# A two-block fp32 transformer kernel on one core: the start reordered, with the stream loaded ahead of the modulation weights and lambda computed first

## The reference, cut to what matters

```python
c_act = jax.nn.silu(c)
mod = c_act @ mod_w[i] + mod_b[i]                     # 1024 -> 6144
sh_m, sc_m, gt_m, sh_f, sc_f, gt_f = jnp.split(mod, 6)
h = rmsnorm(x, norm_pre_mix[i]) * (1.0 + sc_m) + sh_m
y = conformer_conv_module(h, a_pw1_w, ...)            # h @ w1 first: 1024 -> 2048
...
hdn = jnp.sin(freq * (z @ fw1 + fb1))                 # z: 1024 x 33, fw1: 33 x 64
hdn = jnp.sin(freq * (hdn @ fw2 + fb2))               # fw2: 64 x 64
...
lam = exp(sum(lambda_q1 * lambda_k1)) - exp(sum(lambda_q2 * lambda_k2)) + lam_init
a = p[:, :, 0] - lam * p[:, :, 1]                     # in the attention
```

## Time and profile before

| | |
|---|---|
| median of 3 runs | 3311.95 us |
| lowest and highest | 3311.55 and 3317.38 us |
| the profiled execution | 3311.95 us |
| its span | 3310.2 us |
| mean granted TensorE clock | 0.963 of full |
| PE busy | 3096.4 us |
| DVE, ACT, POOL busy | 1656.5, 1011.4, 433.0 us |
| span start to the first pw1 matmul | 61.1 us |

### The profile page before, as it was taken

The page is one execution under the profiler, slowest core; times in us unless marked ns, Lnnn a source line. Parts: engine busy times, 40 slices in busy tenths (PEclk is TensorE's granted clock), DMA queues, the critical chain, the costliest instruction groups (busy, mean ns, idle before and its releaser), DMA issues. The chain is left out here.

```text
span 3310.2 us, 33559 instructions
## 1 busy us (share of the span) xinstructions
PE 3096.4 (94%) x13822; PEld 2500.5 (76%) x13822; DVE 1656.5 (50%) x1752; ACT 1011.4 (31%) x1203; POOL 433.0 (13%) x177
## 2 busy tenths in 40 slices
PE   7897878899999999989999999889999999999996
PEld 3683457778888888768888877678777788888885
DVE  5596765665556564574521066577465413222225
ACT  3444434232222121233221133467232311111111
POOL 0587750000000000000200034000020000000000
PEclk9998888899999999999999999999998999999998
DMA  6113432132323322221332244442332212111112
GB/s 206 51 39 121 159 121 102 64 103 76 91 63 127 102 92 81 102 77 64 124 123 94 99 153 143 118 91 54 105 113 73 75 32 64 45 42 61 39 45 108
DMA packets 96192, 301.24 MB, mean 91 GB/s; under 512 B 11205, under 2 KB 15045, under 8 KB 95847
## 3 DMA queue, kind: packets, MB, share of 16 engines
q1 hardware_dynamic: 96040, 299.09, 27.6%
HBM read 251.34 MB, written 47.71 MB: 90 GB/s over the span
## 5 line engine op out<-in xcount | busy, mean ns | idle before, releaser
L704 PE MATMUL ps<-mainr,wh 128*128 128x512 f32 (+1 forms) x6592 | 1778.5, 390 | 28.8 <-POOL wl L2445 9.7
L704 PEld LDWEIGHTS ps<-mainr,wh 128*128 128x128 f32 x6592 | 1236.5, 189 | 284.4 <-issue 28.0
L704 PE MATMUL ps<-mainr,wl 128*128 128x512 f32 (+1 forms) x3296 | 1029.0, 389 | 0.0
L704 PEld LDWEIGHTS ps<-mainr,wl 128*128 128x128 f32 x3296 | 622.4, 189 | 128.0
L1238 ACT CAST wh<-raw 128x1024 fp32r<-128x1024 f32 (+2 forms) x320 | 281.9, 885 | 749.7 <-PE ps L704 539.0
L1714 DVE TENSOR_TENSOR wl<-raw,wh 128x1024 fp32r<-128x1024 f32 (+2 forms) x256 | 265.4, 1038 | 462.8 <-ACT wh L1238 462.6
L2445 POOL TENSOR_TENSOR wl<-raw,wh 128x1024 fp32r<-128x1024 f32 x64 | 154.2, 2415 | 426.1 <-ACT wh L1238 425.9
L1973 DVE TENSOR_TENSOR mainf<-mainf,ps 128x1024 f32<-128x1024 f32 x80 | 97.6, 1220 | 214.5 <-PE ps L704 214.5
L750 PE MATMUL ps<-mainr,wh 128*128 128x512 f32 x576 | 163.0, 406 | 36.8 <-issue 22.2
L2016 DVE SCALAR_TENSOR_TENSOR ps<-mainf,vec,ps 128x1024 f32<-128x1024 f32 (+1 forms) x174 | 180.9, 1102 | 2.5 <-ACT ps L1426 2.3
L2483 POOL TENSOR_TENSOR tmp<-tmp,mainf 128x1024 f32<-128x1024 f32 x8 | 27.5, 3442 | 1177.0 <-DMA mainf<-in_rope 1114.9
(11 more groups left out here) (232 smaller groups left out, 2872.3 us busy)
## 6 DMA issues: line engine op xcount, KB each, us to landing
raw<-in_mod_w SPq DMA_DIRECT2D x48, 512.0 KB, 4.3
raw<-in_ada_w SPq DMA_DIRECT2D x48, 512.0 KB, 3.6
raw<-in_f_up SPq DMA_DIRECT2D x44, 512.0 KB, 4.3
raw<-in_g_up SPq DMA_DIRECT2D x44, 512.0 KB, 3.5
raw<-in_w_in SPq DMA_DIRECT2D x40, 512.0 KB, 4.1
raw<-in_pw SPq DMA_DIRECT2D x24, 512.0 KB, 3.9
sc_x<-mainf SPq DMA_DIRECT2D x24, 512.0 KB, 2.6
mainf<-sc_x SPq DMA_DIRECT2D x24, 512.0 KB, 6.2
```

The costliest lines, as they stand in the source:

```text
L704: ins = e.matmul(out, wt[:, a:b], xs[n], start=kk == 0 and t == 0, stop=kk == kt - 1 and t == 2)
```

## The change

The orders of all engines but POOL are changed.

- SP: x is issued right after vec and ident, then dbias and lamv; the raw tiles 0 to 3 come behind them. zT, fw1, fw2 and fsmall come after raw tile 11, whose issue waits for raw tile 7 to be consumed.
- PE: blocks 0 and 1, hidden layer 0, block 2, the sums of squares, turns 0 to 2, block 3, turn 3, hidden layer 1, the spread.
- ACT: the two exponentials of lambda come ahead of the squares of x, rows 0 to 2 after them, then the root, row 3, the first sine, the first three weights of pw1.
- DVE: all of lambda comes ahead of the additions of squares; sums 0 to 2 stand together, sum 3 after xxcopy and ahead of the reciprocal; hidden_argument(1) after the reciprocal.
- Planner: the first hidden layer and the column sums are taken ahead of block 3.

The number of instructions of each kind stays as it is, apart from waits and table loads.

```diff
--- before.py
+++ after.py
@@ -540,10 +540,11 @@
         d, acc, tmp = self.d, self.acc, self.tmp
         for i in range(1, ND):
             tmp.take(("x1sq", i), ("x1add", i))
-        for jb in range(4):
+        for jb in range(3):
             self.mod_paired("m", jb)
         self.aux_take(("hid", 0), [("hts", 0)], [("hts", 0)])
         self.aux[0].take(("cols", "x1"), ("sqrt", "n1"), ("xxcopy",))
+        self.mod_paired("m", 3)
         self.aux_take(("hid", 1), [("hts", 1)], [("hts", 1)])
         self.norm_plan("n1")
         acc.only(0, 1, 2)
@@ -942,19 +943,18 @@
 
 
     modulation("m", 0)
+    modulation("m", 1)
     hidden_layer(0)
-    modulation("m", 1)
-    modulation_turn("m", 0)
+    modulation("m", 2)
     w.wait_ge(*k.at("ones", 0))
     w.wait_ge(*k.at("x1add", ND - 1))
     columns(k.S(0), True, True, "x1", 0)
-    modulation("m", 2)
-    modulation_turn("m", 1)
+    for jb in range(3):
+        modulation_turn("m", jb)
+    modulation("m", 3)
+    modulation_turn("m", 3)
     hidden_layer(1)
-    modulation("m", 3)
-    modulation_turn("m", 2)
     norm_spread("n1")
-    modulation_turn("m", 3)
 
 
     x, ready = normed("n1", 8, 16)
@@ -1396,19 +1396,20 @@
     w.wait_ge(*k.at("vec", 0))
     e.activation(k.COL("cact", 0, 8), k.V("c1", 0, 8), ACT.Silu).then_inc(*k.to("cact", 0))
     e.activation(k.COL("cact2", 0, 16), k.V("c2", 0, 16), ACT.Silu).then_inc(*k.to("cact", 1))
+    for n in range(2):
+        w.wait_ge(*k.at("lamsum", n))
+        e.activation(k.COL("lam", n), k.COL("lam", n), ACT.Exp).then_inc(*k.to("lamexp", n))
     for i in range(ND):
         w.wait_ge(*k.at(f"x{i}", "x"))
         if i:
             hold_tmp("x1sq", i)
         e.activation(k.TMP("x1sq", i) if i else k.S(0), k.F(i), ACT.Square).then_inc(*k.to("x1sq", i))
-        if i == 3:
-            modulation_row("m", 0)
-    modulation_row("m", 1)
+    for jb in range(3):
+        modulation_row("m", jb)
     root(("n1",), RMS_EPS, ("cols", "x1", 0))
+    modulation_row("m", 3)
     hidden_sine(0)
-    modulation_row("m", 2)
     split_to(k.W["pw1", 0] + 3)
-    modulation_row("m", 3)
     norm_upper("n1", lambda i: k.R(8 + i), lambda i: k.COL("mod", i))
 
 
@@ -1449,9 +1450,6 @@
             split_to(k.W["pw1", 2 * i + 1] + 3)
         if i == 0:
             hidden_sine(1)
-            for n in range(2):
-                w.wait_ge(*k.at("lamsum", n))
-                e.activation(k.COL("lam", n), k.COL("lam", n), ACT.Exp).then_inc(*k.to("lamexp", n))
         products(POOL_TAPS[i] // 2)
         for t in FIRST_TAPS[i]:
             first_tap(t)
@@ -2085,6 +2083,16 @@
     e.memset(k.COL("sq", 0, 16), 1.0 / 1024).then_inc(*k.to("sq1"))
     for n, v in enumerate(m.eps):
         e.memset(m.eps[v], v).then_inc(*k.to("eps", n))
+    w.wait_ge(*k.at("lam", 0))
+    for n in range(2):
+        pr = m.lamv[:, 128 * n:128 * n + 64]
+        e.tensor_tensor(pr, pr, m.lamv[:, 128 * n + 64:128 * n + 128], ALU.mult).then_inc(*k.to("lammul", n))
+        w.wait_ge(*k.at("lammul", n))
+        e.tensor_reduce(k.COL("lam", n), pr, AX.X, ALU.add).then_inc(*k.to("lamsum", n))
+    w.wait_ge(*k.at("lamexp", 1))
+    e.tensor_tensor(k.COL("nlam"), k.COL("lam", 1), k.COL("lam", 0), ALU.subtract).then_inc(*k.to("nlam", 0))
+    w.wait_ge(*k.at("nlam", 0))
+    e.tensor_scalar(k.COL("nlam"), k.COL("nlam"), -LAM_INIT, None, ALU.add).then_inc(*k.to("nlam", 1))
     for i in range(1, ND):
         w.wait_ge(*k.at("x1sq", i))
         if i > 1:
@@ -2094,16 +2102,16 @@
     hidden_argument(0)
     hidden_reduce(0)
     w.wait_ge(*k.at("vec", 0))
-    modulation_add("m", 0)
+    for jb in range(3):
+        modulation_add("m", jb)
     w.wait_ge(*k.at("cols", "x1", 0))
     w.wait_ge(*k.at("sqrt", "n1"))
     e.tensor_copy(k.COL("xx", 0, 8), m.ps[:, 3072:3080]).then_inc(*k.to("xxcopy"))
+    modulation_add("m", 3)
+    w.wait_ge(*k.at("ident", 0))
     scale(("n1",))
-    modulation_add("m", 1)
+    split_to(k.W["pw1", 0] + 3)
     hidden_argument(1)
-    modulation_add("m", 2)
-    split_to(k.W["pw1", 0] + 3)
-    modulation_add("m", 3)
     hold_mod("m", 3)
     gain(k.COL("gm", 0, 8), k.COL("mod", 8, 8), k.V("npm", 0, 8), "n1")
     norm("n1", lambda i: k.F(i), lambda i: [(f"x{i}", "x")], lambda i: k.COL("mod", i), 8, 16)
@@ -2111,12 +2119,6 @@
 
     turns = vector_turns()
     hidden_reduce(1)
-    w.wait_ge(*k.at("lam", 0))
-    for n in range(2):
-        pr = m.lamv[:, 128 * n:128 * n + 64]
-        e.tensor_tensor(pr, pr, m.lamv[:, 128 * n + 64:128 * n + 128], ALU.mult).then_inc(*k.to("lammul", n))
-        w.wait_ge(*k.at("lammul", n))
-        e.tensor_reduce(k.COL("lam", n), pr, AX.X, ALU.add).then_inc(*k.to("lamsum", n))
     abreast_weights(("pw1", 0))
     for i in range(ND):
         for n in range(2):
@@ -2353,10 +2355,6 @@
         e.scalar_tensor_tensor(out=e1, in0=e1, scalar=k.STAT(n, 5), in1=k.e0_at[n % 2][:, cols], op0=ALU.mult,
                                op1=ALU.add).then_inc(*k.to("atcomb", n, part))
 
-    w.wait_ge(*k.at("lamexp", 1))
-    e.tensor_tensor(k.COL("nlam"), k.COL("lam", 1), k.COL("lam", 0), ALU.subtract).then_inc(*k.to("nlam", 0))
-    w.wait_ge(*k.at("nlam", 0))
-    e.tensor_scalar(k.COL("nlam"), k.COL("nlam"), -LAM_INIT, None, ALU.add).then_inc(*k.to("nlam", 1))
     e.tensor_scalar(k.COL("sub"), k.V("sub"), 1.0 - LAM_INIT, None, ALU.mult).then_inc(*k.to("subg"))
     w.wait_ge(*k.at("nlam", 1))
     w.wait_ge(*k.at("subg"))
@@ -2596,17 +2594,18 @@
 
     e.dma_start(m.vec[:, :], d["vec"]).then_inc(*k.land("vec", 0))
     e.dma_start(m.ident[:, :], d["ident"]).then_inc(*k.land("ident", 0))
-    feed(RAW)
+    for i in range(ND):
+        e.dma_start(k.F(i), d["xT"][i]).then_inc(*k.land(f"x{i}", "x"))
+    e.dma_start(m.dbias[:, :], d["dbias"]).then_inc(*k.land("dbias", 0))
+    e.dma_start(m.lamv[:, :], d["lamv"]).then_inc(*k.land("lam", 0))
+    feed_modulation("m", 0)
+    feed_modulation("m", 1)
     e.dma_start(m.mf[0:33, 24 * SLOT:25 * SLOT], d["zT"]).then_inc(*k.land("fz", 0))
     e.dma_start(m.fw[0:33, 0:64], d["fw1"]).then_inc(*k.land("fw1", 0))
     e.dma_start(m.fw[0:64, 64:128], d["fw2"]).then_inc(*k.land("fw2", 0))
     e.dma_start(m.fw[0:64, 128:131], d["fsmall"]).then_inc(*k.land("fs", 0))
-    for i in range(ND):
-        e.dma_start(k.F(i), d["xT"][i]).then_inc(*k.land(f"x{i}", "x"))
-    for jb in range(4):
-        feed_modulation("m", jb)
-    e.dma_start(m.dbias[:, :], d["dbias"]).then_inc(*k.land("dbias", 0))
-    e.dma_start(m.lamv[:, :], d["lamv"]).then_inc(*k.land("lam", 0))
+    feed_modulation("m", 2)
+    feed_modulation("m", 3)
 
 
     for n in range(2, 2 * ND):
```

## The result

| | before | after | ratio, 95% interval |
|---|---|---|---|
| first comparison | 3314.62 us, 4 runs | 3335.57 us, 4 runs | 1.0065 [1.0053, 1.0078] |
| repeated, on a chip of the experiments | 3318.07 us, 23 runs | 3335.96 us, 6 runs | 1.0049 [1.0036, 1.0061] |

A forecast was written before the change was run, and what follows sets the result against it. PE, busy 94% of the span, bounds the kernel, so pw1's start counts: +10.7 us there less 1.5 from lambda makes +9.2, from 3311.95 to 3321 us. Own range 3317 to 3326; range leaving out 2 in 10 or less 3312 to 3327.

The forecast's parts named there:

- raw tile 0, start of block 0: SP's start: raw tile 0 lands at 18.6 by bytes at 408 GB/s, corrected to 17.6; before it was 6.6.
- blocks 0 and 1: PE: block 0 takes 8.55 after an idle engine, block 1 follows at once at full clock in 6.96, to 33.1.
- the stall ahead of layer 0: PE waits for fw1, issued behind raw tile 11 at about 34.1 and landing 3.4 later: 4.5, ends 3.9 and 5.5.
- layer 0 and block 2: PE behind the stall: 1.86 + 6.96 plus 1.5 for the fallen clock, to 48.0.
- a cooled start costs 1.5: PE's half clock after idleness, priced from block 1 before (8.46 against 6.96); counted once, behind the stall.
- 1.5 more each time: PE's clock falling again in the gaps behind block 2: 1.5 us per fall, none added to the sum.
- rival C: Clock also falls in the turns, layer 1 and the spread: 1.5 to 3.4 more, tile 0 late by 1; up to 3327; chance 0.11.
- fixed cost of 2.0 us: A documentation page's small-transfer cost for fw1: landing at 36.1, the end 1.4 us earlier; the prediction gave it less weight.
- The turns, the sine and hidden_argument ahead of the spread: New critical steps ahead of pw1: three turns in a row 1.6 more, the sine 2.35, hidden_argument 1.33.
- lambda: Table load and exponentials leave the path ahead of the first tap; PE's later waits come 1.5 earlier relative to pw1.
- A: Waits of 2.77 and 8.75 us behind pw1 absorb the delay; kernel no slower, about 3311; chance 0.08.
- B: PE's waits in the new start are covered: fw1 in time, clock held, sine ahead; +1.7 less 1.5, 3312; chance 0.09.

The follow-up runs named there:

- second trace: The changed kernel once more, unchanged, against the kernel before on the same chip as the other experiments; ratio 1.0049 [1.0036, 1.0061].
- filler kernel: The changed kernel plus small 128 x 128 matmuls with unused results in TensorE's gaps from the end of block 1 to pw1; ratio 1.0025 to the kernel before.
- the sine came first: The changed kernel with the first sine ahead of the copy of row 3 on ScalarE; ratio 1.0033 to the kernel before, pw1 at 76.53.
- Early inputs: The changed kernel with zT, fw1, fw2 and fsmall issued right behind raw tiles 0 to 3; ratio 1.0020 to the kernel before, pw1 at 72.58.
- delayed start: The kernel before with 17 memsets on DVE ahead of everything and SP's first transfer waiting for them; ratio 1.0061, about 20 us.
- lambda alone: The kernel before with only lambda moved as in the change, its vectors loaded behind ident; ratio 0.9987 [0.9978, 0.9995].
- fastest version: The kernel before with lambda early, x and raw tiles 4 to 7 interleaved, turns, layer 1, sine and row 3 reordered; 3307.6 against 3319.3 us, ratio 0.9968.

## Why the prediction was wrong

Its own steps, in the order of the new start (forecast, measured, difference in us):

| step | forecast | measured | difference |
|---|---|---|---|
| raw tile 0, start of block 0 | 17.6 | 17.82 | +0.2 |
| blocks 0 and 1 | 15.5 | 16.47 | +1.0 |
| the stall ahead of layer 0 | 4.5 | 5.52 | +1.0 |
| layer 0 and block 2 | 10.3 | 12.28 | +2.0 |
| column sums and three turns | 4.4 | 4.46 | 0 |
| block 3 | 7.0 | 8.72 | +1.7 |
| row 3, turn, sine | 3.0 | 3.23 | +0.2 |
| layer 1 and hidden_argument | 3.4 | 5.08 | +1.7 |
| spread | 2.1 | 3.82 | +1.7 |
| first multiplication to pw1 | 3.9 | 3.88 | 0 |
| sum of the differences | | | +9.5 |

pw1 had been put at 71.8 and came at 81.28. In the second trace it came at 79.64.

**The step that failed is the clock.** The prediction took a cooled start once, "a cooled start costs 1.5", for layer 0 and block 2, and named further falls as "1.5 more each time" without adding any; they stood in rival C, with a chance of 0.11. The trace has half-clock stretches in three places, and beyond the 1.5 that was taken they make 7.1 of the 9.5 us (2.0 + 1.7 + 1.7 + 1.7 in the table). The filler kernel gives 6.8 back at the fallen clock's places without taking a wait away. Two things were wrong. First, the price: 1.5 had been read from one fall, in which only the first 3.1 us of block 1 ran slowly; behind the stall layer 0 and the start of block 2 both paid, 1.7 and 1.7. Second, the count: the falls further down stood at nothing in the sum. The work there is thin: the three turns leave two gaps of 0.72 us, the sine 2.17, DVE 1.43. Layer 1 and the spread ran at full clock when the sine came first, so their waits have a part in it. Block 3's fall can't be put down to its two gaps, since in two other kernels the clock fell without any. What is shown is the falls, their price, and that matmuls in the gaps from 52 us on kept the clock at full in the one trace with them.

**Blocks 0 and 1** were 1.0 slower than forecast, and this is pace again: the slow start of block 0 lasted 5.2 us instead of 3.2, and block 1 ran at full pace throughout. In the traces with x ahead of the raw tiles and this order on PE, the slow start ends after 2.7 to 5.4 us, and the two blocks take 15.2 to 16.6. With it, 8.1 of the 9.5 us are matmuls at half pace.

**The stall** was placed and explained rightly, and 1.0 too short: 3.4 us from the issue of fw1 to landing had been taken, 4.7 passed to PE's start, and the whole stall of 5.52 is at the forecast's own upper end of 5.5. The prediction set a fixed cost of 2.0 us for a small transfer beside this. The Trainium skill states it in "DMA: Bandwidth & Descriptors", section "Anatomy of one DMA — SWDGE (gpsimd) path", for transfers that GpSimd issues. Here SP issued them behind a raw tile, and fw2 (16 KB) took 4.4 us to land, fsmall (0.8 KB) 3.9. Early inputs gave 9.0 back, the stall and its clock.

**Raw tile 0**, by bytes at the full queue's rate less a correction, was right to 0.2; half of the correction, for small packets, was an estimate that no run tests by itself. **The turns, the sine and hidden_argument ahead of the spread** were right in place and size. **lambda** was forecast at 1.5, and 1.65 came back by 161 us.

**The rivals.** A was refuted by the delayed start. B was refuted by the stall. C is what happened, and was too small: block 3, layer 1 and the spread lost 5.1 us to the clock instead of its 1.5 to 3.4, and the fall behind the stall cost another 2.0 more than its price. C's upper end of 3327 is also above what its own terms add up to (3321 + 3.4 + 1 is 3325.4). Take from the delay of 20.2 the extra falls (7.1), the stall (1.0), blocks 0 and 1 (1.0) and what lambda gave back (1.65), and 9.4 is left, against the forecast 9.2.

Not settled: what makes the clock fall in one trace and not in another for the same work, and why lambda alone measured 4 us rather than 1.3.

## What to carry to other kernels

Where a start-up list is thin, price each wait twice: its own length, and TensorE's slow work behind it. Here a stall of 5.5 us cost 9.0, and taking away a wait of 2.2 us for a sine moved pw1 by 4.8. Give the clock a range of its own in the sum, one price (here 1.7 us) for each thin stretch, since some of these falls come in one trace and not in the next. Never queue a small input behind a transfer that itself waits for the work ahead of it. The fastest version also put the small serial steps (a row copy and its transposes, a sine) beside long matmul blocks, and interleaved the loads that share a full queue; what each of these gave by itself was not measured.

## What the runs showed of the hardware

TensorE's granted clock fell in stretches where no single gap was long: in the changed kernel with early inputs block 3 took 9.49 instead of 7.03 behind two gaps of 0.72 us between turns. In the filler kernel it fell as block 2 began (8.72 instead of 7.03), 2 us behind a gap of 1.88 us. It also fell where PE had no gap at all: in the delayed kernel at 54 us, behind a turn of 0.40 and column sums of 1.95 us (block 2 took 8.72), and in the fastest version at 38 us. Where it falls varies from trace to trace: layer 1 of the changed kernel took 3.64 us in one and 1.90 in the other.

Executions of one kernel spread by 3312.8 to 3325.0 us on one chip, so effects of a few microseconds were read from traces first, and two traces of one kernel differed behind pw1's start by 3.8 us (before) and by 5.3 us (the changed kernel, 3252.3 and 3257.7).
